# Two cache units loaded ahead of their ring, and a reordered recurrent loop, in a one-core decoder step

## The reference

```
# recurrent head, prompt in chunks, state c, n
sw  = (q k^T) * exp(d - m)            # d: decay between positions
num = w_inter * (q c) + sw v
den = max(|w_inter * (q n) + sum(sw)|, exp(-m))
hc  = num / den;  hn = hc * rsqrt(mean(hc^2) + eps) * g_head
out = (sigmoid(o) * hn) @ w_out
c_new = a * c + sum_s w_s k_s v_s^T

# attention of the sampled tokens
k_past = cache_k[page_table];  v_past = cache_v[page_table]
p = softmax(q k^T / sqrt(128) - slope * distance);  out = (p v) @ w_out
```

## Time and profile before

| | |
|---|---|
| median of 3 runs | 1279.35 us (1278.76 to 1279.37) |
| profiled execution | 1279.25 us |
| its span | 1277.5 us |
| granted TensorE clock, mean | 0.997 of full |
| TensorE busy | 1247.0 us, 98% |
| VectorE busy | 740.1 us, 58% |
| ScalarE busy | 583.5 us, 46% |
| recurrent section | 317.8 to 380.0 us |
| attention | first prompt scores 960.8, first matmul of the output projection 1004.35 us |

### The profile page before, as it was taken

How to read it: one execution, slowest core, us unless ns; L and a number is a source line. 1 busy time by engine, 2 the same in 40 slices (tenths; PEclk the granted TensorE clock), 3 DMA queues, 4 the chain that set the end, 5 groups by cost and what they waited for, 6 DMA issues and landing times.

```text
span 1277.5 us, 22110 instructions
## 1 busy us (share of the span) xinstructions
PE 1247.0 (98%) x8897; PEld 1222.5 (96%) x8897; DVE 740.1 (58%) x1152; ACT 583.5 (46%) x922; POOL 101.2 (8%) x117
## 2 busy tenths in 40 slices
PE   6999999999999999999999999999998999999996
PEld 6999999999989999999999999999995899999996
DVE  7565654565787656554555565654556576565443
ACT  7454433343455645443434554533443465454332
POOL 3000000100433000000000000000120010000011
PEclk9999999999999999999999999999999999999998
DMA  8434334633333443434543644334448744433441
GB/s 301 165 131 164 103 134 159 212 130 107 134 121 133 165 163 133 144 113 149 186 165 132 239 148 155 131 113 156 171 164 335 293 145 152 156 140 123 136 137 41
DMA packets 35994, 200.50 MB, mean 157 GB/s; under 512 B 4362, under 2 KB 6538, under 8 KB 20450
## 3 DMA queue, kind: packets, MB, share of 16 engines
q1 hardware_dynamic: 33858, 192.34, 42.8%
q0 software_dynamic: 2080, 7.39, 1.8%
HBM read 193.14 MB, written 6.57 MB: 156 GB/s over the span
## 4 chain that ended last, share of the span: by engine, by line
PE 91%; DMA 2%; ACT 2%; issue 2%; DVE 1%; SPq 1%; POOL 0%; POOLq 0%; DVEq 0%; ACTq 0%
PE bank L413 30%; PE bank L414 29%; PE bank L415 29%; DMA raw<-vc_in 1%; ACT w_hi L869 1%; DMA raw<-kc_in 1%; PE bank L523 0%; DMA raw<-w_in 0%; ACT junk L1013 0%; POOL scl L1727 0%; PE bank L534 0%; SPq L389 0%; PE bank L473 0%; ACT ot L1022 0%; DVE x L1670 0%
## 5 line engine op out<-in xcount | busy, mean ns | idle before, releaser
L413 PE MATMUL bank<-h_hi,w_hi 128*128 128x320 f32 x1920 | 598.1, 312 | 11.1 <-DVE h_lo L1210 10.6
L415 PE MATMUL bank<-h_hi,w_lo 128*128 128x320 f32 x1920 | 594.8, 310 | 0.0
L414 PE MATMUL bank<-h_lo,w_hi 128*128 128x320 f32 x1920 | 594.8, 310 | 0.0
L869 ACT ACTIVATE w_hi<-raw 128x1024 fp32r<-128x1024 f32 (+1 forms) x368 | 336.0, 960 | 458.5 <-PE bank L415 454.2
L1198 DVE TENSOR_TENSOR w_lo<-raw,w_hi 128x1024 fp32r<-128x1024 f32 (+1 forms) x368 | 395.6, 1116 | 120.0 <-ACT w_hi L869 119.9
L413 PEld LDWEIGHTS bank<-h_hi,w_hi 128*128 128x128 f32 x1920 | 361.6, 188 | 13.5 <-DVE w_lo L1198 10.6
L414 PEld LDWEIGHTS bank<-h_lo,w_hi 128*128 128x128 f32 x1920 | 361.6, 188 | 0.4
L415 PEld LDWEIGHTS bank<-h_hi,w_lo 128*128 128x128 f32 x1920 | 361.5, 188 | 0.0
L415 PE MATMUL bank<-f_hi,w_lo 128*128 128x320 f32 x704 | 217.7, 309 | 0.0
L414 PE MATMUL bank<-f_lo,w_hi 128*128 128x320 f32 x704 | 217.7, 309 | 0.0
L413 PE MATMUL bank<-f_hi,w_hi 128*128 128x320 f32 x704 | 217.7, 309 | 0.0
(11 more groups left out here) (206 smaller groups left out, 637.1 us busy)
## 6 DMA issues: line engine op xcount, KB each, us to landing
raw<-w_in SPq DMA_DIRECT2D x88, 1024.0 KB, 4.8
raw<-w_out SPq DMA_DIRECT2D x64, 704.0 KB, 4.1
raw<-w_a SPq DMA_DIRECT2D x12, 1024.0 KB, 4.7
raw<-w_kv SPq DMA_DIRECT2D x8, 1024.0 KB, 4.7
raw<-kc_in SPq DMA_DIRECT2D x16, 512.0 KB, 4.5
raw<-vc_in SPq DMA_DIRECT2D x16, 512.0 KB, 7.0
raw<-w_oa SPq DMA_DIRECT2D x4, 1024.0 KB, 5.8
raw<-w_q SPq DMA_DIRECT2D x4, 1024.0 KB, 4.7
```

Source lines behind the costliest of these rows:

```text
L413: pe.matmul(out, wh, mh, start=first, stop=False)
L414: pe.matmul(out, wh, ml, start=False, stop=False)
L415: return pe.matmul(out, wl, mh, start=False, stop=last)
L869: sc.activation(w_hi[:, n_at % 2, part * w:part * w + w], raw[:, raw_of(n_at) % RAW, part * w:part * w + w], ACT.Copy).then_inc(hi_done, 1)
```

## The change

In the recurrent loop VectorE's `outputs` becomes `denominators` and `variances`, with `decay(h+1)` between them, the queries' spreading becomes a function of its own, and `weights(h+1)` goes ahead of `states(h)`. ScalarE runs `decay(h+1)` ahead of `head_scale(h)`. On TensorE the waits for `cp_done`, `kwm_done` and `cn_done` move from the head of `head_outputs` to just before the matmuls that need them.

In attention the key units 0 and 1 leave the ring. SP loads them once unit `U_Q`-1 is multiplied, to a new tensor `page_k`, to 1024 columns of `work` and to `row_room`, which is `row` made 128 partitions high. The other fourteen units go through the four slots. The matmuls of the early units are cut in two, since each page lies by itself.

```
-        row = sb("row", [8, R_COLS])
+        row_room = sb("row_room", [128, R_COLS])
+        row = row_room[0:8, :]
...
+                page_k = sb("page_k", [128, 2048], f32, own)
...
+        early_keys = [[page_k[:, 0:1024], page_k[:, 1024:2048]], [work[:, 1536:2560], row_room[:, 0:1024]]]
...
+        CACHE, EARLY = 2 * NB, 2
+        RING_CACHE = CACHE - EARLY
...
-            return r - U_OB - 1 if U_OB < r <= U_OB + CACHE else None
+            return r - U_OB - 1 + EARLY if U_OB < r <= U_OB + RING_CACHE else None
...
-            for c in range(CACHE):
+            sp.wait_ge(unit_done, U_Q)
+            for c in range(EARLY):
+                for j in range(NPG):
+                    sp.dma_start(early_keys[c][j], page_of(c, j)).then_inc(early_loaded[c], 16)
+            for c in range(EARLY, CACHE):
                 load_cache(c)
...
                 pe.wait_ge(c0_load[h % 2], 16 * (h // 2 + 1))
-                pe.wait_ge(kwm_done, h + 1)
                 if h == 0:
...
                     pe.wait_ge(ot_done, 3 * h)
-                    pe.wait_ge(cp_done, (h + 1) // 2)
-                    pe.wait_ge(cn_done, h)
...
                 if h % 2 == 0:
+                    if h >= 2:
+                        pe.wait_ge(cp_done, h // 2)
...
+                pe.wait_ge(kwm_done, h + 1)
+                if h >= 1:
+                    pe.wait_ge(cn_done, h)
                 for a in range(4):
...
+                    if b < EARLY:
+                        for j in range(NPG):
+                            for k in range(QB):
+                                c = (QB * g + k) * 128
+                                mm = pe.matmul(out[SLOT * k:SLOT * k + SLOT, j * PAGE:j * PAGE + PAGE],
+                                               q_spread[:, QB * g + k, b // 4, own], early_keys[b][j][:, c:c + 128],
+                                               start=False, stop=(b % 4 == 3), skip_group_check=True)
...
                 head_squares(h)
                 if h + 1 < H:
+                    decay(h + 1)
                     head_scale(h)
-                    decay(h + 1)
...
             for h in range(H):
-                outputs(h)
+                denominators(h)
                 if h + 1 < H:
                     decay(h + 1)
+                variances(h)
+                if h + 1 < H:
+                    spread_queries(h + 1)
+                    weights(h + 1)
                     states(h)
-                    weights(h + 1)
```

More of the change, by code:

```diff
@@ L177, in trunk_program @@
         kv_used = sem("cache_unit_used")
+        CACHE, EARLY = 2 * NB, 2
+        early_loaded = [sem(f"early_key_unit_loaded{i}") for i in range(EARLY)]
         pair_free = sem("pair_banks_evacuated")
@@ L284, in trunk_program @@
         U_END = at
-        CACHE = 2 * NB
+        RING_CACHE = CACHE - EARLY
         ORDER = (0, 2, 1, 3)
@@ L303, in cached_at @@
         def cached_at(r):
-            return r - U_OB - 1 if U_OB < r <= U_OB + CACHE else None
+            return r - U_OB - 1 + EARLY if U_OB < r <= U_OB + RING_CACHE else None
         def unit_at(r):
-            return r if r <= U_OB else r - CACHE
+            return r if r <= U_OB else r - RING_CACHE
         def loads_after(r):
@@ L315, in raw_of @@
         def raw_of(n):
-            return n if n <= U_OB else n + CACHE
+            return n if n <= U_OB else n + RING_CACHE
         def raw_of_cache(c):
-            return U_OB + 1 + c
+            return U_OB + 1 + c - EARLY
         def width(n):
@@ L381, in _, with page_of @@
             sp.wait_ge(s_pg, 16)
+            def page_of(c, j):
+                at = NPG * (c % NB) + j
+                page = sp.value_load(pages[0:1, at:at + 1], min_val=0, max_val=kc_in.shape[0] - 1)
+                return (kc_in if c < NB else vc_in)[bass.ds(page, 1), :, :].rearrange("a p c -> p (a c)")
             def load_cache(c):
                 r = raw_of_cache(c)
-                src = kc_in if c < NB else vc_in
                 slot_free(r)
                 for j in range(NPG):
[L388 to L391, removed]
+                    sp.dma_start(raw[:, r % RAW, j * 1024:j * 1024 + 1024], page_of(c, j)
                                  ).then_inc(loaded[r % RAW], 16)
-            for c in range(CACHE):
+            sp.wait_ge(unit_done, U_Q)
[3 more added lines that the diff above has]
+            for c in range(EARLY, CACHE):
                 load_cache(c)
@@ L744, in cache_scores @@
             def cache_scores(b):
-                raw_at = raw_of_cache(b)
-                pe.wait_ge(loaded[raw_at % RAW], loads_after(raw_at))
-                keys = raw[:, raw_at % RAW, :].rearrange("p (g h k) -> p g h k", g=NPG, h=H)
+                if b < EARLY:
+                    pe.wait_ge(early_loaded[b], 16 * NPG)
+                else:
+                    pe.wait_ge(loaded[raw_of_cache(b) % RAW], loads_after(raw_of_cache(b)))
                 own = slice(SLOT * (b % 4), SLOT * (b % 4) + SLOT)
[L750 to L753, removed]
+                for g in range(2):
+                    out = bank[2 * g + b // 4]
+                    if b < EARLY:
+                        for j in range(NPG):
[4 more added lines that the diff above has]
+                                               start=False, stop=(b % 4 == 3), skip_group_check=True)
+                    else:
+                        keys = raw[:, raw_of_cache(b) % RAW, :].rearrange("p (j h k) -> p j h k", j=NPG, h=H)
+                        for k in range(QB):
+                            mm = pe.matmul(out[SLOT * k:SLOT * k + SLOT, 0:PAST], q_spread[:, QB * g + k, b // 4, own],
+                                           keys[:, :, QB * g + k, :], start=False, stop=(b % 4 == 3),
+                                           skip_group_check=True)
                 mm.then_inc(kv_used, 1)
@@ L1400, in decay @@
             def decay(h):
-                hp, r = h // 2, slice(64 * (h % 2), 64 * (h % 2) + 64)
                 ve.wait_ge(head_s, h + 1)
@@ L1408, in decay, with spread_queries @@
                 ins.then_inc(d_done, 1)
+            def spread_queries(h):
+                hp, r = h // 2, slice(64 * (h % 2), 64 * (h % 2) + 64)
                 for half in range(2):
@@ L1419, in weights, with denominators @@
                 ve.tensor_tensor(pmat[:, 0:448], bank[5][:, 0:448], dmat[:, :], ALU.mult).then_inc(p_done, 1)
-            def outputs(h):
+            def denominators(h):
                 o3 = bank[6][:, 0:3 * (DV + 1)].rearrange("p (t d) -> p t d", t=3)
@@ L1428, in outputs, with variances @@
                                  o3[:, :, DV:DV + 1], ALU.max).then_inc(den_done, 1)
+            def variances(h):
                 ve.wait_ge(den_done, h + 1)
@@ L1460, in _ @@
             decay(0)
+            spread_queries(0)
             weights(0)
```

## The result

The changed kernel takes 1274.65 us (median of 7 runs, 1274.27 to 1274.78) where the kernel before took 1279.09 (7 runs, 1278.28 to 1279.76): ratio 0.9965, with a 95% interval of 0.9954 to 0.9977. That is 4.4 us less. Forecast were 1275.3 us and a gain of 4.0. The profiled execution's span is 1272.9 us, 4.6 less than before.

What follows compares the result with a forecast made beforehand. It took VectorE, narrowly, as the bound in heads 3 to 6 and DMA in attention, with TensorE busy 98% of the span. Gains of 1.0 + 3.0 = 4.0 us from 1279.25 gave 1275.3 us, range 1273.8 to 1277.2.

Steps and rivals of the forecast that it cites:

- `pmat` 1.5 us earlier: Recurrent heads, worked out for head 2: `pmat` is ready at 339.1 instead of 340.6, and both 0.51 us waits go.
- `var` and `ot` later, with 0.2 us of cover at the turning: Recurrent heads: `var` 0.45 us later in head 2, `ot` ends 339.97, turning at 340.21; cover 0.2 of 0.7 left.
- Rival A: Recurrent heads: odd heads still lose the port or cover fails, TensorE awaits `ot`; Part 1 is 0, 1276.3 us; chance 0.15.
- The collision: Recurrent heads, `w_lo` against GpSimd's `c0` load and `kwm`: `w_lo` starts just ahead of the `c0` issue, margins 0.1 us.
- D: Recurrent heads: `w_lo` loses to `kwm` in every head, 8.75 us of VectorE per head; 1281.6 us; chance 0.04.
- Part 1: New order of the recurrent heads: 1.3 us of removed waits less 0.3 for moved waits, 1.0 us gained.
- the 0.3 us for waits in the middle of short matmuls: Recurrent heads, TensorE's moved waits: 0.04 us per head, 0.3 in all, set against the gain.
- Part 2: Attention, two key units loaded ahead of the ring: 3.0 us gained, bounds 1.6 and 3.6.
- ring loads then follow the same pattern: Attention: with two units fewer, unit n+2 lands when unit n did, plus 2.0 us.
- rival B: Attention: DMA stays the bound, restart costs over 2.0 us, value waits return; Part 2 is 1.6, 1276.7 us; chance 0.11.
- The early pages cost nothing: Before attention: early pages issued 932.2 to 936.6, where nothing waits for a load; without that cover each costs 1.3 us.
- C: Attention: early units do nothing, the restart slips 5.1 us; only Part 1 is left, 1278.3 us; chance 0.05.

Runs made afterwards that it cites:

- no_act_swap: The changed kernel, but ScalarE runs `head_scale(h)` before `decay(h+1)` as it did; 1279.70 us, ratio 1.0004 to the kernel before.
- kwm_first: The kernel before, but GpSimd makes `kwm` of two heads on before it stores `cn` and loads `c0`; 1277.84 us, ratio 0.9991.
- waits_at_head: The changed kernel with TensorE's waits for `cp_done`, `kwm_done` and `cn_done` back at the head of `head_outputs`; 1274.29 us, ratio 0.9961 to the kernel before.
- early_only: The kernel before plus the two early key units alone, recurrent part old; 1276.22 us, ratio 0.9976.
- heads_only: The kernel before plus the recurrent part of the change alone, all sixteen cache units through the ring; 1277.45 us, ratio 0.9986.

## Why the prediction held, step by step

**`pmat` 1.5 us earlier.** Right. From head 2's denominators to `pmat` it was 3.91 us (336.10 to 340.01) and is 2.47 (335.59 to 338.06).

**`var` and `ot` later, with 0.2 us of cover at the turning.** Right: `ot` ends 0.25 us before the turning of head 2, and 0.24 to 0.25 in each head from 0 to 6. Rival A didn't come. (Its "`ot` was never awaited before" is not quite so: in the kernel before the turnings of heads 4 and 6, behind the two delayed splits, start 0.05 to 0.06 us after `ot` has ended, the same distance as behind `pmat`.) no_act_swap shows what the order costs without its half on ScalarE.

**The collision.** `w_lo` was to start just ahead of the `c0` issue and so to run at once. It does both: it starts 0.05 us ahead in odd heads and 0.12 in even ones, and takes 1.22 to 1.23 in all, so rivals A and D didn't come. But the reason given was wrong. In the kernel before no such `w_lo` starts ahead of the `c0` issue. It starts 0.11, 0.03, 0.11, 0.03 and 0.10 us behind it in heads 1 to 5, and in 1, 2 and 4 it ran at once from there. Head 1 has the starts of head 3 to within 0.01 us and the other outcome (kernel before, GpSimd, then VectorE):

```profile
332.83 0.56 POOL L1734 DMA_DIRECT2D c<-c_in  x1
333.41 1.66 POOL L1717 TENSOR_TENSOR kwm<-kw,con 64x512 f32<-64x512 f32 x1
```

```profile
332.94 1.23 DVE L1198 TENSOR_TENSOR w_lo<-raw,w_hi 128x1024 fp32r<-128x1024 f32 x1 [0.33 <-ACT w_hi L869]
```

And kwm_first shows that the issue of `c0` ahead of `w_lo` does nothing by itself; the collision is with `kwm`. What the kernels here show is this: where `kwm` starts 0.52 us or more behind `w_lo`, `w_lo` ran at once, every time; at 0.46 us it went both ways. The changed kernel has 0.62 to 0.68. The outcome was as forecast, but in part by luck: the margin of 0.1 us that was watched isn't the one that matters, and what decides at 0.46 us stays open.

**Part 1, 1.0 us.** Too low, measured 1.8 in the trace and 1.7 in time. Two terms were mis-sized. The first: "a head costs TensorE 7.63 us where it has no wait". It doesn't, the heads now take 7.49 and 7.68 in turn, 7.59 in the mean. Before, head 3's outputs began 0.05 us after `pmat` had ended (340.69 for 340.64), and no wait was listed for it, as worked out under kwm_first. From head 0 to head 4 it took 30.57 us (317.66 to 348.23) and now takes 30.28; from there to head 7 it took 24.35 and now takes 22.85, 1.5 for my 1.3. The second: the 0.3 us for waits in the middle of short matmuls, which waits_at_head puts at zero; of what was read at L612 as the price of satisfied waits, 0.05 us in each odd head belongs to `pmat`, which wasn't ready. Both errors point the same way: 0.3 us in heads 0 to 3, 0.2 in heads 4 to 6 and 0.3 for the waits are the 0.8 that were missing.

**Part 2, 3.0 us.** Measured 2.4 in the trace of the changed kernel, 2.6 in early_only, and 2.9 in the time of early_only, inside the bounds of 1.6 to 3.6. Unit 6 landed 11.3 us after the first prompt scores (970.0), where I had 11.1. The step that is too good is "ring loads then follow the same pattern". Unit 7's slot is freed by unit 3, which stands behind the first turning and the next scores, where unit 5 before had the slot of unit 1, free at once. So SP stood still and issued its pages at 966.8 and 967.9, where a row of pages behind that of 964.8 would have them at 965.9 and 967.0:

```profile
L398 SPq DMA_DIRECT2D raw<-kc_in x2: 333/333/333, 966.8 to 967.9; - x2
```

Unit 7 landed 3.6 us behind unit 6, and unit 10 another 3.8 behind unit 9; I had one such gap, of 3.8. Units 10 to 15 landed 0.7 to 1.0 us later than worked out, and unit 10's wait of 1.03 us is that. It is rival B at a part of its price. Two of the signs named didn't come: value waits are 2.1 us in sum where under 0.8 was forecast, and the output projection begins 41.15 us after the first prompt scores, not 40.6.

**The early pages cost nothing.** Right: issued 931.2 to 934.5, landed by 939.7, no new wait there: from head 7's outputs to the first prompt scores it takes 588.24 us in the changed kernel and the same in heads_only, which has no early pages. The two early units took 1.77 us on TensorE (960.14 to 961.91) for the 1.87 of two units before.

**The sum.** Part 1 was 0.7 to 0.8 us too low and Part 2 0.1 to 0.6 too high: 4.0 for 4.4, with part of the errors cancelling. Rivals C and D are excluded by the trace and by the two halves' times.

The Trainium skill (SBUF — State Buffer, Who interferes with whom) says that whichever of the two issues first gets the shared port for the whole instruction. By the starts that a trace shows, the changed kernel agrees in heads 1 to 5 (`kwm` 1.45 to 1.51 us beside `w_lo`, for 1.05 alone). Heads 3 and 5 of the kernel before don't: there `w_lo` had the earlier start and lost. The Trainium skill (DMA: Bandwidth & Descriptors, Where 436 GB/s comes from) gives about 358 GB/s, half of a stack's bandwidth for each of two cores, as what binds such loads. In this kernel, on one core, the trace still disagrees: units land each 2.55 us at the end, 411 GB/s.

## What to carry to other kernels

When two instructions swap places on one engine, look at what each needs from another engine and swap there too, or leave both. A wait that no list shows can still cost 0.15 us in every second round of a loop: compare the starts of the rounds, and look whether an instruction always starts at the same short distance behind the end of what it needs. Where a ring's transfers are the bound, ask when the first slots come free after the stage begins, and find memory that is idle just at that moment; the first unit taken out of the ring brought most of the gain, the second little, and closing the standstill 1.1 us more.

## What was not expected of the hardware

The landing of value unit 10 varied from run to run of the same attention: TensorE waited 1.03, 0.92, 0.80, 0.34 and 1.24 us for it, with attention between 40.46 and 41.35 us. In the changed kernel its two pages were issued at 973.4 and 974.5, the first page of unit 11 at 976.1:

```profile
L398 SPq DMA_DIRECT2D raw<-vc_in x2: 333/333/333, 973.4 to 974.5; - x2
...
DMA to landing us min/median/max: 6.6/7.3/8.0
```

```profile
L398 SPq DMA_DIRECT2D raw<-vc_in x1: 333/333/333, 976.1 to 976.1; - x1
...
DMA to landing us min/median/max: 6.5/6.5/6.5
```

The page issued at 974.5 took 8.0 us and landed at 982.5, the one issued at 976.1 took 6.5 and landed at 982.6. Up to then pages landed one after the other, 1.3 us apart; from then on the second page of a unit and the first of the next land together, each 2.55 us. The engines move as much as before (419 GB/s in the 2.7 us up to 978.7, 406 from 980.0 to 982.55), but the page that TensorE waits for lands with one that nobody needs yet, and all units behind it are late once by about the 1.25 us of a page. That the two pages share the engines is read from these landings; no run tests it. The same step shows before the change between units 5 and 6 (3.8 us apart, for 2.57). What decides at which unit it happens wasn't tested.
